# Gate and up weights of the experts loaded as 512 features by 1024 columns instead of 1024 by 512

## The reference

```
def _moe(h, w_router, w_gate, w_up, w_down):
    """Top-2-of-8 SwiGLU experts, softmax over the selected logits, sorted grouped dispatch."""
    ...
    xs = xf[tok_sorted]
    group_sizes = jnp.bincount(flat_e, length=N_EXPERTS).astype(jnp.int32)
    hid = jax.nn.silu(lax.ragged_dot(xs, w_gate, group_sizes)) * lax.ragged_dot(xs, w_up, group_sizes)
    ys = lax.ragged_dot(hid, w_down, group_sizes)
    ys = ys * gates.reshape(-1)[order][:, None].astype(ys.dtype)
    out = jnp.zeros_like(xf).at[tok_sorted].add(ys)
    return out.reshape(B, S, D)
```

## Time and profile before

| | us |
|---|---|
| median of 3 runs | 1930.48 |
| lowest and highest run | 1927.61 and 1934.44 |
| the profiled execution's own time | 1927.14 |
| its span in the profile | 1925.4 |
| TensorE (PE) busy in the span | 1853.1 (96%) |
| VectorE (DVE), ScalarE (ACT), GpSimd (POOL) busy | 416.6, 288.4, 88.0 |
| experts: from the first wide matmul to the last matmul of down | 970.65 to about 1903 |

### The profile page before, as it was taken

How to read it: one execution, slowest core, us unless ns; L and a number is a source line. 1 busy time by engine, 2 the same in 40 slices (tenths; PEclk the granted TensorE clock), 3 DMA queues, 4 the chain that set the end, 5 groups by cost and what they waited for, 6 DMA issues and landing times. The chain is left out here.

```text
span 1925.4 us, 28536 instructions
## 1 busy us (share of the span) xinstructions
PE 1853.1 (96%) x12786; PEld 922.1 (48%) x12786; DVE 416.6 (22%) x829; ACT 288.4 (15%) x570; POOL 88.0 (5%) x127
## 2 busy tenths in 40 slices
PE   7999998999999999999899999999999999999996
PEld 4476664456644454557444444443444444444442
DVE  2533333223610000236321010111101011010121
ACT  1210221223310000232211010110101011010110
POOL 0010000004100000023000000000000000000000
PEclk9999999999999999999999999999999999999998
DMA  9742118344224352432669999999999999999991
GB/s 278 241 154 90 45 66 301 129 145 164 88 87 175 119 188 91 168 131 93 224 239 390 390 378 398 381 392 387 373 390 367 403 387 375 387 369 398 390 401 69
DMA packets 222548, 492.87 MB, mean 256 GB/s; under 512 B 14547, under 2 KB 26451, under 8 KB 222292
## 3 DMA queue, kind: packets, MB, share of 16 engines
q1 hardware_dynamic: 213783, 477.00, 68.1%
q10 hardware_dynamic: 6702, 7.03, 1.2%
q0 software_dynamic: 1936, 6.95, 0.9%
HBM read 480.72 MB, written 12.98 MB: 256 GB/s over the span
## 5 line engine op out<-in xcount | busy, mean ns | idle before, releaser
L1284 PE MATMUL bank<-ring,work 128*128 128x512 f32 (+4 forms) x1632 | 673.0, 571 | 18.5 <-ACT work L1498 3.6
L1284 PEld LDWEIGHTS bank<-ring,work 128*128 128x128 f32 x1632 | 305.7, 192 | 357.5 <-issue 324.2
L2798 PE MATMUL bank<-ring,work 128*64 128x512 f32 x1792 | 394.0, 596 | 3.7 <-DMA ring<-in_moe_w_up 3.0
L2798 PEld LDWEIGHTS bank<-ring,work 128*64 128x64 f32 x1792 | 127.7, 137 | 248.8 <-issue 248.0
L2809 PE MATMUL bank<-ring,work 128*32 128x256 f32 x3584 | 201.8, 382 | 2.7 <-DMA ring<-in_moe_w_up 2.7
L2850 PE MATMUL bank<-ring,work 128*64 128x512 f32 x896 | 199.3, 596 | 0.0
L2809 PEld LDWEIGHTS bank<-ring,work 128*32 128x32 f32 x3584 | 113.9, 110 | 101.2 <-issue 30.8
L2968 DVE TENSOR_TENSOR work<-work,bank 64x512 f32<-64x512 f32 x56 | 38.7, 692 | 374.3 <-ACT work L2890 374.3
L2850 PEld LDWEIGHTS bank<-ring,work 128*64 128x64 f32 x896 | 61.5, 137 | 120.9 <-issue 120.9
L2860 PE MATMUL bank<-ring,work 128*32 128x256 f32 x1792 | 103.3, 381 | 0.0
L2890 ACT ACTIVATE work<-bank 64x512 f32<-64x512 f32 x56 | 33.0, 589 | 365.8 <-PE bank L2798 365.8
(11 more groups left out here) (371 smaller groups left out, 1151.8 us busy)
## 6 DMA issues: line engine op xcount, KB each, us to landing
ring<-in_moe_w_gate SPq DMA_DIRECT2D x56, 2048.0 KB, 19.8
ring<-in_moe_w_up SPq DMA_DIRECT2D x56, 2048.0 KB, 18.4
ring<-in_moe_w_down SPq DMA_DIRECT2D x56, 2048.0 KB, 19.6
ring<-in_w_in SPq DMA_DIRECT2D x20, 2048.0 KB, 8.3
ring<-in_w_out SPq DMA_DIRECT2D x6, 2048.0 KB, 8.3
ring<-in_dense_w_gate SPq DMA_DIRECT2D x5, 2048.0 KB, 7.8
ring<-in_dense_w_up SPq DMA_DIRECT2D x5, 2048.0 KB, 7.8
ring<-in_dense_w_down SPq DMA_DIRECT2D x5, 2048.0 KB, 7.8
```

The lines of the kernel that those rows point to most:

```text
L1284: mm = pe.matmul(banks(j)[:, 0:width], x[:, k0 + kt, tt * P:(tt + 1) * P], w[:, kt, c0:c0 + width], start=first and n == 0, stop=last and ...
L2798: mm = pe.matmul(out[half, :], xgT[:, k, 0:64], w[n][:, k, :], start=(k == 0), stop=(k == KD - 1))
```

## The change: what it does

Gate and up weights of chunks 0 to 5 are loaded by pairs of chunks (`PAIRS` = 3). A load is one half of the input features (512) by the 1024 columns of both chunks: 4 pieces of 4 KB per partition, in place of 8 of 2 KB. Its bytes, the number of loads and the slots are the same; only chunk 6, which has no partner, keeps the old shape. The order is gate and up of half 0, then gate and up of half 1.

A pair is computed half by half: with half 0 wide of both chunks and then narrow of both, with half 1 narrow of both and then wide of both. So sums of four groups are open at once. Wide sums of four chunks get banks of their own (0, 1, 6, 7; the last two are shared with the results of `down`), and the narrow sums of a pair share one bank, side by side. `hid` has four buffers instead of three. Transposes of a pair stand behind the narrow form of half 1 of the next pair; those of chunks 4 and 5 now both stand behind chunk 6. ScalarE and VectorE follow that order. The first seven loads of the first expert, which are issued before the stage begins, have the new shape too.

```
 def pair_weight(a, e, i):
+    w = a[("moe_w_gate_2", "moe_w_up_2")[i % 2]][0, e]
+    if i < 4 * PAIRS:
+        p, half = i // 4, i % 4 // 2
+        return w[half * BANK:(half + 1) * BANK, p * DM:(p + 1) * DM].rearrange("(k p) n -> p k n", p=P)
+    if i < 2 * NC:
+        return w[:, PAIRS * DM:EF].rearrange("(k p) n -> p k n", p=P)
+    return expert_weight(a, e, i)
...
-    hid = [take(BANK) for _ in range(3)]
+    hid = [take(BANK) for _ in range(4)]
...
+    wide_of = lambda c: (ps[0], ps[1], ps[6], ps[7])[c % 4]
+    narrow_of = lambda c: narrow_out[c // 2 % 2][:, 256 * (c % 2):256 * (c % 2) + 256]
...
-                sp.dma_start(expert_slot(core, i), expert_weight(a, e, i)).then_inc(core.landed[slot_of(core, i)], 16)
+                sp.dma_start(pair_slot(core, i), pair_weight(a, e, i)).then_inc(core.landed[slot_of(core, i)], 16)
...
+            def pair(e, p):
+                chunks = range(2 * p, min(2 * p + 2, NC))
+                halves = 2 if p < PAIRS else 1
+                if p == 0:
                     pe.wait_ge(xg_ready, e + 1)
+                for half in range(halves):
+                    i = 4 * p + 2 * half
                     landed(e, i)
+                    landed(e, i + 1)
+                    w = [pair_slot(core, i), pair_slot(core, i + 1)]
+                    for form in (pair_wide, pair_narrow)[::-1 if half else 1]:
+                        for c in chunks:
+                            form(e, c, w, half, halves)
+                        if half and form is pair_narrow and p:
+                            for c in range(2 * p - 2, 2 * p):
+                                turn_chunk(e, c)
+                    pending[0] += 2
...
+                if half == 0 and c >= 4:
+                    pe.wait_ge(hid64, NC * e + c - 3)
+                elif half == 0 and c >= 2 and e:
+                    pe.wait_ge(ys_by_vector, e)
+                    pe.wait_ge(ys_by_scalar, e)
...
-                for c in range(NC):
-                    chunk(e, c)
+                for p in range(PAIRS + 1):
+                    pair(e, p)
+                turn_chunk(e, NC - 3)
                 turn_chunk(e, NC - 2)
```

More of the change, by code:

```diff
@@ L2672 @@
 LOADS = 3 * NC
+PAIRS = NC // 2
 def expert_weight(a, e, i):
@@ L2689, in expert_slot, with pair_weight, pair_slot @@
     return core.ring[:, slot_of(core, i), :].rearrange("p (k n) -> p k n", n=BANK if i < 2 * NC else DM)
+def pair_weight(a, e, i):
+    w = a[("moe_w_gate_2", "moe_w_up_2")[i % 2]][0, e]
[5 more added lines that the diff above has]
+    return expert_weight(a, e, i)
+def pair_slot(core, i):
+    return core.ring[:, slot_of(core, i), :].rearrange("p (k n) -> p k n", n=BANK if 4 * PAIRS <= i < 2 * NC else DM)
 def experts_first(core, a, r, xn, gain):
@@ L2762, in gather @@
                     pe.wait_ge(hid32, NC * e - 1)
-                for j, bank in enumerate((wide_out[x], narrow_out[x])):
+                for j, bank in enumerate((wide_out[0], narrow_out[0])):
                     for k in range(4):
@@ L2775, in gather @@
                     mm.then_inc(gathered, 1)
-            def chunk(e, c):
-                if c == 0:
+            def pair(e, p):
+                chunks = range(2 * p, min(2 * p + 2, NC))
+                halves = 2 if p < PAIRS else 1
+                if p == 0:
                     pe.wait_ge(xg_ready, e + 1)
-                for i in (2 * c, 2 * c + 1):
+                for half in range(halves):
+                    i = 4 * p + 2 * half
                     landed(e, i)
[L2784 to L2798, removed]
+                    landed(e, i + 1)
[6 more added lines that the diff above has]
+                                turn_chunk(e, c)
@@ new lines, in pair, with pair_wide @@
+                    pending[0] += 2
+            def pair_wide(e, c, w, half, halves):
+                out, cols = wide_of(c), slice(c % 2 * BANK, (c % 2 + 1) * BANK)
+                tiles = KD // halves
+                if half == 0 and c >= 4:
[3 more added lines that the diff above has]
+                    pe.wait_ge(ys_by_scalar, e)
+                for k in range(tiles):
+                    last = half == halves - 1 and k == tiles - 1
+                    for n, rows in enumerate((lower, upper)):
+                        mm = pe.matmul(out[rows, :], xgT[:, half * tiles + k, 0:64], w[n][:, k, cols],
+                                       start=(half == 0 and k == 0), stop=last)
@@ L2799, in chunk_wide, with pair_narrow @@
                         give_back(mm)
-                        if k == KD - 1:
+                        if last:
                             mm.then_inc((gate64, up64)[n], 1)
[L2803 to L2807, removed]
+            def pair_narrow(e, c, w, half, halves):
+                out, first, tiles = narrow_of(c), c % 2 * BANK, KD // halves
+                alone = halves == 1
+                if half == 0 and c in (4, 6):
+                    pe.wait_ge(hid32, NC * e + c - 2)
+                for k in range(tiles):
+                    last = half == halves - 1 and k == tiles - 1 and (alone or c % 2 == 1)
@@ L2808, in chunk_narrow @@
                     for q in range(4):
-                        mm = pe.matmul(narrow[quarter[q], 0:256], xgT[:, k, 64:96],
-                                       w[q // 2][:, k, (q % 2) * 256:(q % 2 + 1) * 256], start=(k == 0), stop=(k == KD - 1))
+                        cols = slice(first + q % 2 * 256, first + q % 2 * 256 + 256)
+                        mm = pe.matmul(out[quarter[q], :], xgT[:, half * tiles + k, 64:96], w[q // 2][:, k, cols],
+                                       start=(half == 0 and k == 0 and c % 2 == 0), stop=last, skip_group_check=not alone)
@@ L2811, in chunk_narrow @@
                         give_back(mm)
-                        if k == KD - 1 and q % 2 == 1:
-                            mm.then_inc((gate32, up32)[q // 2], 1)
+                        if last and q % 2 == 1:
+                            mm.then_inc((gate32, up32)[q // 2], 1 if alone else 2)
             def turn_chunk(e, c):
@@ L2823, in turn_chunk @@
                 for k in range(4):
-                    mm = pe.transpose(turn_out[c % 2][:, k * P:(k + 1) * P], hid[g % 3][:, k * P:(k + 1) * P], ident)
+                    mm = pe.transpose(turn_out[c % 2][:, k * P:(k + 1) * P], hid[g % 4][:, k * P:(k + 1) * P], ident)
                     give_back(mm)
@@ L2895, in silu_narrow @@
                         act.wait_ge(hid32, g - 1)
-                    nc.scalar.activation(sil[g % 2][upper, BANK:BANK + 256], narrow_out[g % 2][lower, 0:256], ACT.Silu)\
+                    nc.scalar.activation(sil[g % 2][upper, BANK:BANK + 256], narrow_of(g % NC)[lower, :], ACT.Silu)\
                       .then_inc(silu32, 1)
[L2899 to L2908, removed]
+                for p in range(PAIRS):
+                    g = NC * e + 2 * p
+                    silu_narrow(g)
+                    silu_narrow(g + 1)
+                    if p:
+                        copy_turned(2 * p - 2)
+                        copy_turned(2 * p - 1)
+                    silu_wide(g)
+                    silu_wide(g + 1)
+                silu_wide(NC * e + NC - 1)
+                silu_narrow(NC * e + NC - 1)
+                copy_turned(NC - 3)
                 copy_turned(NC - 2)
@@ L2955, in take_gathered @@
             def take_gathered(e):
-                x = (NC * e) % 2
-                for j, bank in enumerate((wide_out[x], narrow_out[x])):
+                for j, bank in enumerate((wide_out[0], narrow_out[0])):
                     dve.wait_ge(gathered, 2 * e + j + 1)
@@ L2967, in times_wide @@
                 dve.wait_ge(up64, g + 1)
-                dve.tensor_tensor(hid[g % 3][upper, :], sil[g % 2][upper, 0:BANK], wide_out[g % 2][upper, :], ALU.mult)\
+                dve.tensor_tensor(hid[g % 4][upper, :], sil[g % 2][upper, 0:BANK], wide_of(g % NC)[upper, :], ALU.mult)\
                    .then_inc(hid64, 1)
@@ L2974, in times_narrow @@
                 for q in range(2, 4):
-                    last = dve.tensor_tensor(hid[g % 3][0:32, (q - 2) * 256:(q - 1) * 256],
+                    last = dve.tensor_tensor(hid[g % 4][0:32, (q - 2) * 256:(q - 1) * 256],
                                              sil[g % 2][quarter[q], BANK:BANK + 256],
-                                             narrow_out[g % 2][quarter[q], 0:256], ALU.mult)
+                                             narrow_of(g % NC)[quarter[q], :], ALU.mult)
                 last.then_inc(hid32, 1)
@@ L3019, in _ @@
             for e in range(NE):
[L3020 to L3026, removed]
+                for p in range(PAIRS + 1):
+                    chunks = [NC * e + c for c in range(2 * p, min(2 * p + 2, NC))]
+                    for form in (times_narrow, times_wide)[::1 if p < PAIRS else -1]:
+                        for g in chunks:
+                            if g >= 4:
+                                dve.wait_ge(turned, g - 3)
```

(8 more changed lines are left out.)

9 lines of the change are left out of this document (3 added, 6 removed).

## The result

| | before | changed |
|---|---|---|
| median of 5 runs, us | 1930.48 | 1917.55 |
| lowest and highest | 1925.0 and 1934.44 | 1914.22 and 1917.75 |
| the profiled execution and its span | 1927.14, 1925.4 | 1914.22, 1912.4 |
| the experts' stage in the trace | 933.50 | 919.94 |

The ratio is 0.9929, with an interval of 0.9913 to 0.9946: the change makes the kernel faster by 0.5 to 0.9%. The forecast was 1918 us.

What follows compares the result with a forecast made beforehand. TensorE and DMA were both taken as full in the experts' stage, with DMA slightly short. From 1927.1 us, -9.8 for loads and -1.0 for order gave 1916.3; allowing for the median's 3.3 us offset, 1918 us, range 1914 to 1929.

Steps and rivals of the forecast that it cites:

- Which of the two gives way: Experts' stage: TensorE and DMA both full; at 384 GB/s an expert's bytes take 116.7 us, 1.4 more than TensorE.
- The loads, -9.8 us: Experts 4 to 7: waits for loads and the slowed stretches behind them go with 4 KB pieces, -9.8 us.
- the account of an expert: DMA time per expert: loads 108.2 us plus 5.2 for small transfers and dips, 113.4 against TensorE's 115.3.
- The packet's fixed part, 14 ns: Loads' queue: 85 ns per 2 KB packet against 155 per 4 KB, so about 14 ns do not depend on length.
- The rule that was weighed: Gate and up loads: about 3 cycles overhead a packet would give 4 KB packets only 1.023 times the rate, 397 GB/s.
- Order on TensorE, -1.0 us: Experts' stage: the order of matmul runs adds no term; moved transposes give -0.07 in seven experts, -0.50 in the last.
- -0.07 in seven experts: Transposes: first group gone, -0.50; group behind chunk 6 grows by four, +0.43; wait taken as covered by transposes and gathering.
- From the profiled execution to the median: The median lies 3.3 us above the profiled execution; if waits, that goes, else 1919.6; forecast set between, 1918 us.
- Half the speed: Rival, chance 0.12: 4 KB gate and up pieces reach only 398 GB/s, perhaps half the 9.8 us stays; 1923 us.
- no difference: Rival, chance 0.14: rate depends on lying in one DRAM run; 388 GB/s and waits stay, only transposes gain; 1929.5 us.
- slower: Rival, chance 0.08: longer pieces from a strided tensor run worse; at 376 GB/s +16 us, 1946 us.
- a DMA share below 1: Sign in the changed kernel's profile: DMA share falls below 1 within the experts' stage, or SP waits for slots throughout.

Runs made afterwards that it cites:

- order-alone kernel: The changed kernel with every gate and up load in the old shape, pieces of 2 KB: 1927.98 us, ratio 0.9986.
- loads-alone kernel: The kernel before, its TensorE order kept, with the changed kernel's 4 KB loads for chunks 0 to 5: 1921.12 us, ratio 0.9962.
- the kernel bound by them: The changed kernel without most of its narrow matmuls, so that TensorE is done before the loads: 1882.1 us.
- kernel with short pieces in one run: The kernel before with each gate or up load taken from 2 MB of consecutive DRAM addresses, in pieces of 2 KB: 1932.0 us, ratio 1.0006.

## Why the prediction was right, and where it was not

**Which of the two gives way: right.** The balance of 388.7 GB/s needed and 384 delivered said that TensorE runs into the loads in the late experts. The order-alone kernel is the test of it: it needs 44.8 MB in 114.84 us, 390 GB/s, gets 383 to 386 in experts 4 to 6, and is slower there by 1.6 to 2.1 us each than with wide loads, where 1 to 2% are missing.

**The loads, -9.8 us: right, in size too.** The loads-alone kernel has a stage 9.87 us shorter; its median is 8.3 us below before's. The choice of 409 GB/s for strided pieces of 4 KB held (409 with TensorE out of the way, 408 in the changed kernel from 1025 to 1040 us), and so did the account of an expert: 113.4 us expected from loads of 5.13 and 5.40 us and 5.2 for the rest, 111.3 to 113.4 measured in the kernel bound by them. That a wait can cost a slower clock behind it as well is in the same number: the three waits of before are 5.7 us of the 9.8. But it does not follow every wait. Behind 2.66 us of waiting the narrow run took 5.27 us instead of 3.66 and the granted clock was 0.51 from 1818 to 1820 us; in the kernel with short pieces in one run, the wait at the same place left the run as it was, and the clock at 1.00 from 1829 to 1831 us:

```profile
1829.12 3.66 PE L2818 MATMUL bank<-ring,work 128*32 128x256 f32 x64 [2.69 <-DMA ring<-in_moe_w_up]
```

The waits of 1.3 to 1.5 us in the order-alone kernel had no slow run behind them either. What decides it, no run here shows.

**The packet's fixed part, 14 ns: too large.** From the three speeds a packet of 2, 4 and 8 KB takes 16 x 2048 / 387 = 84.7, 160 and 311 ns (the speeds being 387, 409 and 421 GB/s). That is 75.5 ns more for each 2048 bytes, so by this estimate 9.2 ns are fixed. I had 14 because I gave this queue's 2 KB packets all of the 45 us, while other queues moved 0.45 MB in the same stretch:

```profile
DMA packets 8546, 17.45 MB, mean 388 GB/s; under 512 B 144, under 2 KB 144, under 8 KB 8542
```

With the whole speed, 16 x 2017 / 388 = 83.2 ns a packet, the two rows of before give 9 as well. It did not enter the sum.

**The rule that was weighed** against it, of the Trainium skill, "DMA: Bandwidth & Descriptors", "Why small descriptors are slow (HBM only)", about 3 cycles a packet, would have made the step 1.023. It is 409 / 387 = 1.057, so here the measurement decides against the rule's size. The Trainium skill, same page, "Specifications", names a ceiling of 435 GB/s for the fabric. With the fixed part taken off, the three speeds here tend to 16 x 2048 / 75.5 = 434 GB/s, an estimate that agrees; the fastest stretch above had 421.

**Order on TensorE, -1.0 us: too small, it was -3.7.** The step that failed is "-0.07 in seven experts". I took the stretch of the gathering, 0.97 us, as its cost, and so took the wait as covered, while 0.30 of it was the very wait that I asked about. The gathering's modelled end (1047.18 + 0.83) hides 0.16 of it, and the 0.14 behind that the row does not name. The last expert's row, with 0.81 us of idle time and the same 1.46 us, told it: the transposes began 1.46 or 1.47 us after the narrow matmuls with and without a gathering in between, which is the mark of a wait and not of work. An expert gains 0.48 us, so 0.41 more than I had. Beside the 0.30 most of the rest is this: the change from narrow to wide costs the same whether transposes stand between or not (7.04 us for the 128 narrow ones both times), where I had added 0.08. In the last expert -0.5 was about right (116.37 to 115.79).

**From the profiled execution to the median: unfounded.** I took half of the 3.3 us between them as waits for loads that would go. In the changed kernel, which has none, the median is again 3.3 us above the profiled execution; when it ran again it was 0.7 above, and in the loads-alone kernel 5.7 below. So the distance says only which execution the profiler happened to take. With the order's measured size, and nothing taken off for this, the sum is 1930.5 - 9.8 - 3.7 = 1917.0. That the forecast of 1918 lay within half a microsecond of 1917.55 is in part luck: 2.7 us too little for the order stood against 1.7 us taken off without ground. What held is the mechanism and its main term.

**The rivals.** Half the speed, no difference and slower each ask for another speed than 409 GB/s while pairs are loaded, and fall by that one number. Of the signs, a DMA share below 1 did not come while experts 1 to 6 ran (1.01 to 1.03), although TensorE no longer waited for loads: an expert's loads need 111.3 to 113.4 of its 114.84 us, so little is spare.

## What to carry to other kernels

When two resources are both full, compare what one needs with what the other delivers over a whole period, not their busy shares: a lack of 1% showed here as a few waits late in the stage, some of them with a slow stretch behind. Before reordering work on the engine, see whether the loads can take longer pieces. And where work stands between a producer and its consumer, compare the interval with and without that work: if it does not change, it is a wait, whatever the idle column says.

## What I had not expected of the hardware

The speed of a load depended on the length of its pieces and not on whether they lie in one run, and pieces of 8 KB (421 GB/s) went faster than those of 4 KB (409 GB/s), as one packet each.

The other surprise is where the runs differ. The stage begins at 970.65 us in the trace of before, at 970.97 and 973.48 in two of the changed kernel, and at 974.15, 975.29, 980.29 and 982.52 in others whose program ahead of it has the same work. The profiled execution of the loads-alone kernel took 1926.78 us with no wait for a load, since its stage began 9.6 us later. The granted clock from 150 to 200 us was 0.93 there and 1.00 in the trace of before; whether that clock is the cause or follows from something ahead was not tried. Within the stage the changed kernel, which does not wait for loads, repeats to the hundredth (919.94 us twice), while its two profiled executions are 2.3 us apart and their stages begin 2.5 us apart. So for a change of half a percent the stage's own length in the trace tells more than the time of the runs. For the kernel before, whose stage has waits, there is one trace (933.50 us; the kernel with the same order and short pieces in one run had 931.94), and no run shows how much its stage varies.
